# A decoder layer on one core: the joined reorderings, and the recurrence's rows summed apart in the output projection

## What is computed

```python
u = rmsnorm(x, norm_attn)
proj = u @ w_in                                  # q, k, v, indexer, z, x/B/C, dt
att = att_fn(q, k, v, qi, wi, ki)                # 8 heads, sparse, 1024 rows
y, h_fin = ssd_scan(xs, dt, A, Bm, Cm, h0, chunk)    # 16 heads of the recurrence, 1024 rows
y = rmsnorm(y.reshape(B, T, SSM_WIDTH) * jax.nn.silu(z), ssm_norm)
h = x + jnp.concatenate([att, y], axis=-1) @ w_out
f = rmsnorm(h, norm_ffn)
h = h + (jax.nn.silu(f @ w_gate) * (f @ w_up)) @ w_down
```

## Time and profile before

| | us |
|---|---|
| median of 3 runs | 2797.06 (2794.6 to 2797.34) |
| the profiled execution | 2797.83 |
| its span, first to last instruction | 2796.0 |
| TensorE busy | 2698.8 |
| VectorE busy | 1797.4 |
| ScalarE busy | 1034.1 |
| GpSimd busy | 393.2 |

### The profile page before, as it was taken

One profiled execution on the slowest core, in us unless ns is written; L12 is line 12 of the kernel. 1 busy time (PEld: TensorE's weight loads), 2 busy tenths in 40 slices (PEclk: granted clock), 3 DMA queues, 4 the chain that ended last, 5 costly groups with the idle time before them and its releaser, 6 DMA issues.

```text
span 2796.0 us, 49441 instructions
## 1 busy us (share of the span) xinstructions
PE 2698.8 (97%) x20313; PEld 2607.2 (93%) x20313; DVE 1797.4 (64%) x2593; ACT 1034.1 (37%) x1538; POOL 393.2 (14%) x166
## 2 busy tenths in 40 slices
PE   8999999999999879999999999999999999899997
PEld 7988999888888769989999999999999999899996
DVE  3333699566566562458777777777777777777423
ACT  5233222333333342344343434434333443533223
POOL 2322333222222113320000000000000000000231
PEclk9999999999999989999999999999999999999998
DMA  6322222666666663423334333333433554645521
GB/s 224 124 77 82 96 93 85 173 177 178 189 179 189 178 208 112 142 86 108 124 118 143 110 125 116 116 117 117 135 109 108 188 158 153 241 142 164 203 107 68
DMA packets 394992, 388.94 MB, mean 139 GB/s; under 512 B 25949, under 2 KB 355269, under 8 KB 391704
## 3 DMA queue, kind: packets, MB, share of 16 engines
q1 hardware_dynamic: 375976, 364.33, 41.4%
q10 hardware_dynamic: 18800, 21.58, 2.2%
HBM read 319.11 MB, written 68.00 MB: 138 GB/s over the span
## 4 chain that ended last, share of the span: by engine, by line
PE 70%; issue 13%; DVE 6%; POOL 5%; DMA 2%; SPq 2%; ACT 1%; ACTq 0%; POOLq 0%; DVEq 0%
PE PS L1452 44%; PE PS L946 14%; PE PS L1436 5%; POOL WL L830 4%; PE PS L1148 1%; DVE mt L2307 1%; DVE ex L2299 1%; SPq L553 1%; DVE WL L2465 1%; PE PS L1387 1%; PE PS L1188 0%; DMA WRAW<-in_w_out 0%; PE PS L1177 0%; DVE xo_t L2614 0%; PE PS L1344 0%
## 5 line engine op out<-in xcount | busy, mean ns | idle before, releaser
L1452 PE MATMUL PS<-xo_t,WH 128*128 128x288 f32 x2544 | 516.0, 297 | 14.4 <-DVE WL L2465 4.0
L946 PE MATMUL PS<-AH,WH 128*128 128x288 f32 (+1 forms) x2144 | 481.2, 306 | 6.6 <-POOL WL L860 2.6
L946 PE MATMUL PS<-AH,WL 128*128 128x288 f32 (+1 forms) x2144 | 462.1, 297 | 0.0
L946 PE MATMUL PS<-AL,WH 128*128 128x288 f32 (+1 forms) x2144 | 461.5, 297 | 0.0
L1452 PEld LDWEIGHTS PS<-xo_t,WH 128*128 128x128 f32 x2544 | 411.7, 190 | 16.1 <-issue 16.1
L1452 PE MATMUL PS<-xo_x,WH 128*128 128x288 f32 x1936 | 389.3, 295 | 2.3 <-DVE xo_x L2553 1.0
L946 PEld LDWEIGHTS PS<-AH,WH 128*128 128x128 f32 (+1 forms) x2144 | 345.9, 190 | 37.0 <-issue 34.9
L1452 PE MATMUL PS<-xo_t,WL 128*128 128x288 f32 x1272 | 377.1, 296 | 0.0
L946 PEld LDWEIGHTS PS<-AH,WL 128*128 128x128 f32 (+1 forms) x2144 | 347.8, 190 | 0.0
L946 PEld LDWEIGHTS PS<-AL,WH 128*128 128x128 f32 (+1 forms) x2144 | 347.5, 190 | 0.0
L2465 DVE TENSOR_TENSOR WL<-WRAW,WH 128x1024 fp32r<-128x1024 f32 x201 | 245.8, 1223 | 109.1 <-ACT WH L1884 107.9
(11 more groups left out here) (393 smaller groups left out, 3762.5 us busy)
## 6 DMA issues: line engine op xcount, KB each, us to landing
WRAW<-in_w_gate SPq DMA_DIRECT2D x22, 2048.0 KB
WRAW<-in_w_up SPq DMA_DIRECT2D x22, 2048.0 KB
WRAW<-in_w_down SPq DMA_DIRECT2D x32, 1024.0 KB
WRAW<-in_w_in SPq DMA_DIRECT2D x14, 2048.0 KB, 8.1
raw<-in_w_in SPq DMA_DIRECT2D x48, 512.0 KB, 4.6
vca<-in_cache_v SPq DMA_DIRECT2D x256, 64.0 KB, 2.7
WRAW<-in_w_out SPq DMA_DIRECT2D x16, 1024.0 KB, 8.0
kca<-in_cache_k SPq DMA_DIRECT2D x232, 64.0 KB, 2.0
```

The lines of the kernel that those rows point to most:

```text
L946: last = nc.tensor.matmul(G[gslot][0:width, h, 0:HALF], wt[:, half if slot is None else slot, k % 8, 0:width], act[:, k, h * HALF:(h + 1) ...
L1452: last = mm(out, wt[:, k, :], act[:, m, k, :], start=(j in (0, 1, 3) and k == 0 and wt is wh and m == 0), stop=(k == 7 and wt is wl), skip ...
```

## The change

Several edits come together.

- The recurrence rows get sums of their own: `M`, two pairs of PSUM banks. `mamba_step` and the new `out_half` add blocks 8 to 15 into M, blocks 0 to 7 into G. The gain is applied where a block is cast and subtracted. The inverse root `rm` is applied per tile: VectorE multiplies M by it, adds G to `xt`, and adds the two: three operations where one was.
- The ninth pass is reordered. The first half of the first output weights and mixed rows 0 and 1 are loaded in pass 7. The last states get a buffer of their own, `h0x`, so that the second half of these weights doesn't wait for the states' store. On ScalarE the decays' exponentials come behind the copies of xtok and of two key blocks and behind the cast of the first weights; other casts move too. Recurrence steps begin inside the pass.
- The first weights of tile 2 are cast earlier (`C3 + 4`).
- At the two exchanges of factors two columns are interleaved in `seq`, the factors are turned at the places in `NEED`, the second column keeps its parts in `kept2`, and its weights are loaded between factors 3 and 4.
- In `load_mamba` the small loads change order.

The diff, context lines left out:

```diff
@@ -177,6 +177,7
+h0x = sb("h0x", [P, NB, P], at=spot["AH"][0] + 14 * NT * 4)
@@ -188,6 +189,7
+rm = sb("rm", [P, 2, HALF], at=spot["kept"][0])
@@ -200,6 +202,7
+kept2 = sb("kept2", [P, 3, HALF], at=spot["us2"][1])
@@ -220,6 +223,7
+M = [PS[:, 6:8, :], PS[:, 4:6, :]]
@@ -376,6 +380,10
+NEED = (0, 1, 2, 4, 6, 8, 10)
+for q in FIRST:
+    seq[7 * q:7 * q + 14] = [(q, 0), (q, 1), (q, 2), (q + 1, 0), (q, 3), (q + 1, 1), (q, 4), (q + 1, 2), (q, 5), (q + 1, 3), (q, 6),
+                             (q + 1, 4), (q + 1, 5), (q + 1, 6)]
@@ -530,20 +538,21
-one(sp.dma_start(sz[:, :], rows(zS, i)))
...
+for e in range(2):
     one(sp.dma_start(dcol[e * DS:(e + 1) * DS, :], bass.AP(I["d_skip"].tensor, i * 2 + e, [[0, DS], [1, 1]])))
+one(sp.dma_start(sz[:, :], rows(zS, i)))
-sp.dma_start(h0[:, :, :], bass.AP(I["state_ssm"].tensor, i * (P * P), [[P, P], [NM * DS * P, NB], [1, P]])).then_inc(s["h0_in"], 16)
+sp.dma_start((h0x if i == 7 else h0)[:, :, :], bass.AP(I["state_ssm"].tensor, i * (P * P), [[P, P], [NM * DS * P, NB], [1, P]])).then_inc(s["h0_in"], 16)
-sp.dma_start(bass.AP(O["ssm_sample"].tensor, (i - 1) * (P * P), [[P, P], [NM * DS * P, NB], [1, P]]), h0[:, :, :]).then_inc(s["hout"], 16)
+sp.dma_start(bass.AP(O["ssm_sample"].tensor, (i - 1) * (P * P), [[P, P], [NM * DS * P, NB], [1, P]]), (h0x if i == 8 else h0)[:, :, :]).then_inc(s["hout"], 16)
@@ -569,25 +578,26
-    sp.wait_ge(s["mixa"], 16 * 6)
-    load_mix(0, 0, 6)
+    sp.wait_ge(mx_in[0], 16)
+    load_mix(0, 2, 6)
-    sp.wait_ge(s["w_lo"], C3)
-    sp.dma_start(first[:, 0:8, :], wo_v[:, 0:8, 0:256]).then_inc(mx_in[2], 16)
+    load_states(a)
-if a > 0:
+if a > 0 and units:
+    sp.wait_ge(s["hout"], 16 * 7)
+    sp.dma_start(first[:, 8:16, :], wo_v[:, 8:16, 0:256]).then_inc(w_ld[0], 32)
-    sp.wait_ge(mx_in[0], 16)
+    sp.wait_ge(mx_in[0], 32)
@@ -613,9 +623,13
+sp.wait_ge(s["w_lo"], C3)
+sp.dma_start(first[:, 0:8, :], wo_v[:, 0:8, 0:256]).then_inc(mx_in[2], 16)
+sp.wait_ge(s["mixa"], 16 * 6)
+load_mix(0, 0, 2)
@@ -667,8 +681,6
-sp.wait_ge(s["hout"], 16 * 8)
-sp.dma_start(first[:, 8:16, :], wo_v[:, 8:16, 0:256]).then_inc(w_ld[0], 32)
@@ -767,14 +779,14
+if j == 3:
+    load_weights(q + 1)
-load_weights(q + 1)
-load_weights(q + 1)
@@ -840,7 +852,7
-act.wait_ge(s["w_used"], c - 1)
+act.wait_ge(s["w_used"], c - (2 if isinstance(c, int) and c == C3 + 4 else 1))
@@ -930,6 +942,12
+def kept_in(q):
+    return kept2 if q - 1 in FIRST else kept
+MIX_AT = {j: n for n, j in enumerate((0, 1, 2, 3, 4, 5, 6, 8, 9, 10, 11, 12, 7, 13, 14, 15))}
@@ -1196,6 +1214,27
+def mamba_step(d, k):
+    wh, wl = (W3[:, 0, :, :], W3[:, 1, :, :]) if d == 0 else (WH[:, 1, :, :], WL[:, 1, :, :])
+    pe.wait_ge(s["w_lo"], C3 + d + 3)
+    pe.wait_ge(s["mix_lo"], MIX_AT[k] + 1)
+    for wt, act in ((wh, AH), (wh, AL), (wl, AH)):
+        for h in range(2):
+            last = mm(M[d][:, h, 0:HALF], wt[:, k - 8, :], act[:, k, h * HALF:(h + 1) * HALF], start=(k == 8 and wt is wh and act is AH), stop=(k == KT - 1 and wt is wl))
+    if k == KT - 1:
+        last.then_inc(s["w_used"], 1)
+def out_half(n, half):
+    pe.wait_ge(s["w_lo"], C3 + 2 * n + half + 1)
+    for k in range(8 * half, 8 * half + 8):
+        for wt, act in ((WH, AH), (WH, AL), (WL, AH)):
+            for h in range(2):
+                last = mm((M[n % 2] if half else G[(T3 + n) % 2])[:, h, 0:HALF], wt[:, half, k % 8, :], act[:, k, h * HALF:(h + 1) * HALF],
+                          start=(k % 8 == 0 and wt is WH and act is AH), stop=(k % 8 == 7 and wt is WL))
+    last.then_inc(s["w_used"], 1)
@@ -1203,11 +1242,11
-pe.wait_ge(s["mix_lo"], k + 1)
+pe.wait_ge(s["mix_lo"], MIX_AT[k] + 1)
-                  start=(k == 0 and wt is WH and act is AH), stop=False)
+                  start=(k == 0 and wt is WH and act is AH), stop=(k == 7 and wt is WL))
@@ -1345,10 +1384,15
-for k in range(6):
+for k in range(3):
-out_step(1, 6)
+for k in range(3, 7):
+    out_step(1, k)
+tgiven(pe, "pv3", i)
+tgiven(pe, "us0", i)
+for k in range(8, 11):
+    mamba_step(0, k)
@@ -1400,27 +1444,16
-def mamba_step(d, k):
-    wh, wl = (W3[:, 0, :, :], W3[:, 1, :, :]) if d == 0 else (WH[:, 1, :, :], WL[:, 1, :, :])
-    pe.wait_ge(s["w_lo"], C3 + d + 3)
-    pe.wait_ge(s["mix_lo"], k + 1)
-    for wt, act in ((wh, AH), (wh, AL), (wl, AH)):
-        for h in range(2):
-            last = mm(G[(T3 + d) % 2][:, h, 0:HALF], wt[:, k - 8, :], act[:, k, h * HALF:(h + 1) * HALF], start=False, stop=(k == KT - 1 and wt is wl))
-    if k == KT - 1:
-        last.then_inc(s["w_used"], 1)
-for k in range(8, 12):
+for k in range(11, KT):
-for k in range(12, KT):
-    mamba_step(1, k - 4)
-    mamba_step(0, k)
-for k in range(12, KT):
+tgiven(pe, "us1", 8)
+tgiven(pe, "ats", 8)
+for k in range(8, KT):
-        half_unit(pe, C3 + 2 * n + h, h, (T3 + n) % 2)
+        out_half(n, h)
@@ -1709,12 +1742,17
-elif j == 6:
-    act.wait_ge(mx_in[0], 32)
-elif j < 6:
-    act.wait_ge(mx_in[0], 16)
+elif j < 7:
+    act.wait_ge(mx_in[0], 16 if j < 2 else 32 if j < 6 else 48)
-    act.wait_ge(s["y_norm"], j - 7)
+    if j == 8:
+        act.wait_ge(mx_in[1], 16)
+    if j == 14:
+        act.wait_ge(s["hout"], 16 * 8)
+    if j == 15:
+        act.wait_ge(s["y_done"], 8)
+    actv(AH[:, j, :], mixed(j), ACT.Copy, scale=gains[:, 24 + j:25 + j]).then_inc(s["m_hi"], 1)
+    return
@@ -1731,11 +1769,16
-act.wait_ge(s["ssm_in"], LOADS * i)
-actv(ea[:, :], ea[:, :], ACT.Exp).then_inc(s["ea_done"], 1)
-for e in range(2):
-    ins = actv(elt[:, e, :].rearrange("p (c j) -> p c j", j=1), abc[:, e, 0:NP].rearrange("p (c j) -> p c j", j=P)[:, :, P - 1:P], ACT.Exp)
-    ins.then_inc(s["ea_done"], 1)
+def decays():
+    act.wait_ge(s["ssm_in"], LOADS * i)
+    actv(ea[:, :], ea[:, :], ACT.Exp).then_inc(s["ea_done"], 1)
+    for e in range(2):
+        ins = actv(elt[:, e, :].rearrange("p (c j) -> p c j", j=1), abc[:, e, 0:NP].rearrange("p (c j) -> p c j", j=P)[:, :, P - 1:P], ACT.Exp)
+        ins.then_inc(s["ea_done"], 1)
+if units:
+    decays()
@@ -1743,6 +1786,9
+if not units:
+    hi_p(C3, 0, 0, 0)
+    decays()
@@ -1750,10 +1796,6
-else:
-    mix_high(0)
-    mix_high(1)
-    hi_p(C3, 0, 0, 0)
@@ -1762,8 +1804,8
-mix_high(2)
-mix_high(3)
+for j in range(4):
+    mix_high(j)
@@ -1782,6 +1824,8
+if not units:
+    hi_p(C3 + 1, 2, 0, 1)
@@ -1822,12 +1866,18
-    hi_p(C3 + 1, 2, 0, 1)
+    act.wait_ge(s["lg_done"], 5 * 7 + 5)
+    hi_p(C3 + 2, ATT_FIRST[2], 0, 3)
+    for j in range(8, 11):
+        mix_high(j)
+if not units:
+    for j in range(11, 13):
+        mix_high(j)
@@ -1847,13 +1897,10
-mix_high(7)
-act.wait_ge(s["lg_done"], 5 * 7 + 5)
-hi_p(C3 + 2, ATT_FIRST[2], 0, 3)
-mix_high(8)
+for j in (7, 13, 14, 15):
+    mix_high(j)
-for j in range(9, KT):
-    mix_high(j)
+hi_p(C3 + 4, 0, 1)
@@ -1887,9 +1934,13
-if q:
+if q == FIRST[0] + 1:
+    act.wait_ge(s["t_st"], 16 * 16)
+elif q == FIRST[1] + 1:
+    act.wait_ge(s["e_add"], ADD[FIRST[0] + 1, 6])
+elif q:
-copy(kept[:, n, :], F[up][:, BANK[j], 0:HALF]).then_inc(s["e_cp"], 1)
+copy(kept_in(q)[:, n, :], F[up][:, BANK[j], 0:HALF]).then_inc(s["e_cp"], 1)
@@ -1906,7 +1957,7
-if c >= 4:
+if c >= 5:
@@ -1946,8 +1997,8
-j = n + 4
-if 0 <= j < 7:
+if n + 4 in NEED:
+    j = NEED.index(n + 4)
@@ -2317,7 +2368,10
-dve.wait_ge(s["m_hi"], j + 1)
+dve.wait_ge(s["m_hi"], MIX_AT[j] + 1)
+if j >= 8:
+    stt(AL[:, j, :], mixed(j), gains[:, 24 + j:25 + j], AH[:, j, :].bitcast(F32), ALU.mult, ALU.subtract).then_inc(s["mix_lo"], 1)
+    return
@@ -2368,6 +2419,9
+if not units:
+    for j in range(2):
+        mix_low(j)
@@ -2413,42 +2467,34
+        for j in range(8, 11):
+            mix_low(j)
+    hs = h0x if i == 8 else h0
-            ins = stt(h0[:, 4 * g + b, :], h0[:, 4 * g + b, :], els[:, 4 * g + b:4 * g + b + 1], bank(f"us{g}")[:, b * P:(b + 1) * P], ALU.mult, ALU.add)
+            ins = stt(hs[:, 4 * g + b, :], hs[:, 4 * g + b, :], els[:, 4 * g + b:4 * g + b + 1], bank(f"us{g}")[:, b * P:(b + 1) * P], ALU.mult, ALU.add)
-    if not units:
-        dve.wait_ge(s["ssy_taken"], 2)
-        nc.vector.reciprocal(rstd[:, 0, :], rstd[:, 0, :])
-    if not units:
-        nc.vector.reciprocal(rstd[:, 1, :], rstd[:, 1, :]).then_inc(s["ry_done"], 1)
-def y_norm(j):
-    v = mixed(j)
-    if j == 8:
-        dve.wait_ge(mx_in[1], 16)
-    if j == 15:
-        dve.wait_ge(s["ymix"], 16 * 8)
-    stt(v, v, gains[:, 24 + j:25 + j], rstd[:, :, :].rearrange("p a b -> p (a b)"), ALU.mult, ALU.mult).then_inc(s["y_norm"], 1)
+for j in (11, 12, 7, 13, 14, 15):
+    mix_low(j)
+dve.wait_ge(s["ssy_taken"], 2)
+nc.vector.reciprocal(rm[:, 0, :], rstd[:, 0, :])
+nc.vector.reciprocal(rm[:, 1, :], rstd[:, 1, :]).then_inc(s["ry_done"], 1)
-for j in range(8, KT):
-    y_norm(j)
-    mix_low(j - 1)
-mix_low(KT - 1)
@@ -2578,8 +2624,11
-x = xt[:, n % 2, :]
-tt(two(x), G[(T3 + n) % 2][:, :, 0:HALF], two(x), ALU.add).then_inc(s["tile_taken"], 1)
+x, part = xt[:, n % 2, :], sqf[:, n % 2, :]
+tt(two(part), M[n % 2][:, :, 0:HALF], rm[:, :, :], ALU.mult).then_inc(s["y_norm"], 1)
```

(3 more changed lines are left out.)

17 lines of the change are left out of this document (7 added, 10 removed).

## The result

The changed kernel takes 2778.46 us (median of 4 runs, 2776.5 to 2780.41), the kernel before 2797.2 us beside it: a ratio of 0.9935, with a 95% interval of 0.9918 to 0.9952. That is 18.7 us less, under one per cent but clear of the noise; 24.5 us, to 2773 us, were forecast. The profiled execution took 2780.41 us, with a span of 2778.1.

A forecast was written before the change was run, and what follows sets the result against it. TensorE was taken as the bound, busy 2698.8 of 2796.0 us, leaving idle and low-clock stretches to win. Last pass 19 plus switches 6 less 0.5 behind the last output tile gave 24.5 us: about 2773 us, range 2762 to 2785.

The forecast's parts named there:

- The last pass: Seventh pass's first state update to third output tile: 19 us gained from earlier loads, moved casts and dropped normalisations; bounds 12 to 23.
- the slow start: Start of the third output tile, before at a low clock: 1.7 us of surplus busy time, counted within the 19 us.
- 2 us of new idle: First output step in the last pass: TensorE waits 2 us for its low part, made by VectorE after four weighings.
- The 14 us at clock 0.74 give back about 2 us: Early last pass: after a shorter wait TensorE's step runs at the full clock rate, gaining about 2 us.
- Then the mixed rows 8 to 14 come last: End of the last pass: these rows land at 1010 us, decode row follows at 1017, TensorE waits some 3 us.
- The output projection: Output tiles: VectorE's two more operations a tile cost 0 inside the slack; 0.5 us (0 to 1.5) behind the last tile.
- The switches: Two exchanges of the down product's seven factors: interleaving gains 3.5 us each, less 0.5 each for loads: 6 us, bounds 0 to 26.
- the loss follows the overhang: At both switches TensorE's loss tracks VectorE's work beyond its spare time, 11.7 us before, 8.2 after: 3.5 us gained each.
- (1): Rival: mixed rows or a clock drop hold the last pass, switches give nothing: 2787 us; chance 0.14 together with (4).
- (2): Rival: interleaving removes nearly all of the switches' loss, 20 us there: 2758 us; chance 0.08.
- (3): Rival: output projection's per-tile chain breaks, TensorE stops in each of 14 tiles beyond 2.9 us of slip: 2807 us; chance 0.04.
- (4): Rival: separate recurrence sums do nothing, mixed rows still last after the old chain's length: 2790 us; chance 0.14 together with (1).

The follow-up runs named there:

- second execution: Another profiled execution of the changed kernel, with no further edit; its last pass took 79.88 us and its span was 2775.0 us.

## Why the prediction was right, and where it was off

**The last pass: right in place, 2 us too large.** Forecast 17.3 us (19 less the slow start), measured 15.2 and 14.8, with a scatter of some 2 us.
- The transposes of the sample keys came at 980.91 us, 978.4 in the time scale of before (the entry's 2.5 us taken off): forecast 978. Undoing the early load and its cast makes the pass 9.2 us longer, where this step was forecast at 8.
- The "2 us of new idle" of the first output step came out at 1.2 us (no wait before). In the forecast this and the next term cancel; as both are smaller than forecast, the sum is little the worse for it, and that is luck. The new wait for btok was foreseen in kind ("only the copies of btok stand behind it now") and not as a price; it is part of the 978.4.
- "The 14 us at clock 0.74 give back about 2 us": in the profiled execution this term failed. Busy time is 68.35 before and 67.99 after. The mean granted clock of the stretch rose from 0.86 to 0.89 only. In the second execution (clock 0.91) 2.2 us were given back, but its idle time was 2.3 us longer. With one trace of the kernel before, a clock term of 2 us can be neither shown nor ruled out.
- "Then the mixed rows 8 to 14 come last": wrong. SP issued them at 1005.02 us, they took 7.7 us to land, 1012.7, and ScalarE came to their casts at 1014.34 without waiting. What was late was ScalarE's own queue ahead of these casts, and then VectorE beside GpSimd (with the split later the wait for the decode row falls to 0.9 us). The decode row began at 1022.38 us, 1019.9 in the scale of before, where 1017 was forecast, and the wait for it was 2.23 us, forecast 3. The price of this step was nearly right for another reason. Behind it the 22 steps took 17.76 us (19.28 in the second execution), forecast 17.6 and 1 us of handoffs.
- "The order of the pass's small loads ... 0, at most 0.5 us": the early second half of the weights in front of the seventh mixed row makes ScalarE wait 1.25 us; this instruction was not in the sum, and what that costs the pass can't be told from the scatter.

**The slow start of the third tile.** Forecast 1.7 less 0.5 for the join; measured 1.5 for both (1175.80 to 1174.27 us). Up to the join TensorE was busy for 180.9 us before and is for 179.4 now, so the start gives nearly all of it. At the join it waits 2.37 us, 0.92 before, and the next waits are shorter by about as much (2.28 us, before 1.01 and 3.26): that is covered, and the 0.5 us were not needed.

**The output projection: right.** 2.61 us for the addition, the cast on time, tiles at full rate. The slack held three additions more but for 1.8 us, and not eight.

**The switches: 4.0 us (2.5 to 4.1 with the scatter), forecast 6.** The failed step is "the loss follows the overhang". The overhang was put 3.5 us smaller at each switch, the time fell by 1.6 and 2.4. Three things were left out. The seven low parts are not spread evenly over 11 products: the first three still fall on three products in a row, and the waits in front of P1 and P2 are what they were (2.38 and 2.38 us, 3.19 and 3.27). Ahead of P2 VectorE isn't short of time but stands still, for a cast behind a load, in both kernels (2.42 us). And at the first switch the rows to be added to come last as soon as VectorE is less late. The forecast saw that load ("SP stands in that wait ...") and priced it at 0.5 us; they land 9.6 us after their issue, 4.9 before, and moving the low part from behind them gives back 1.3.

**Together.** The forecast span is 2796.0 - 24.5 = 2771.5 us, the profiled one 2778.1. The 6.6 us between them are 2.2 in the last pass, 2.2 in the switches and 2.5 in front of the last pass, less 0.3 at the projection. The second execution, without the late entry, has a span of 2775.0 us.

**The rivals.** (1) falls with the last pass and (2) with the order put back. (3) is real, but needs more additions than the change has. (4), that the separate sums bring nothing, wanted 2790 us, 12 more than measured, and a pass that still ends after the old chain's length, where its part behind the decode row is 7 to 8.6 us shorter. But that part has several edits, and no run takes the sums out alone: what they give by themselves is open.

## What to carry to other kernels

When an idle time is taken out, add up the idle time of the stage and not the single waits of the list: a wait of 5.0 us was worth about 3, because another of 2.9 us came in its place, and two edits on one wait don't add up. When an engine in order is the bound over a short stretch, look at which of its instructions stand behind one that waits for something else; a step taken from in front of one wait can land in front of a worse one, as the postponed low parts did. When loads are moved forward, ask which small load then stands behind them. An addition of two SBUF rows on VectorE beside a GpSimd subtraction is to be priced at up to GpSimd's length (2.6 us, not 0.76), and costs nothing as long as the consumer has that much room.

## What was not expected of the hardware

- The same code can take the same time by accident. Both traces of the changed kernel have a last pass of 79.5 to 79.9 us, but its two parts differ by 1.1 and 1.5 us in opposite senses, the second through the clock. Cutting a stage at one more event shows which differences are firm: from P2 to the end nine traces agree to 0.1 us, from P1 to P2 they scatter by 1.4, up to the last pass by 6.9, while the totals differ by some 3 us from run to run.
- VectorE's additions beside GpSimd are held up once and not each, in the two tiles looked at: three more took 4.18 us together, eight 8.41, that is 1.9 and 2.3 us more than at 0.76 each, where one subtraction of GpSimd takes 2.4.
- Less idle time is not always what a better order gives: with the low parts ahead of the additions TensorE stood still no shorter between P1 and P2 and was busy 1.8 us less.
